# Four copies of an expert tile's code in TensorE's loop, put in the order widest first

## The chip, the cores and the metric

The kernel runs on one core of one Trainium2 chip. The metric is the device time of one execution in microseconds (us). Before the change the median of 3 runs is 2206.23 us, from 2205.37 to 2207.76 us.

## The reference

One encoder block on 1024 tokens of 1024 channels, in float32. A token mixer (gated short convolution beside multi-head latent attention, one output projection) is followed by a mixture of experts: the router picks 4 of 32 experts for each token, each expert is a clamped SwiGLU of width 1024, and the outputs are added, weighted by the gates.

```python
def moe_ffn(h, w_router, b_router, w_gate_up, b_gate_up, w_down, b_down):
    logits = hf @ w_router + b_router
    top_vals, top_idx = lax.top_k(logits, TOP_K)          # 4 of 32
    gates = jax.nn.softmax(top_vals, axis=-1)
    order = jnp.argsort(top_idx.reshape(-1))              # token rows sorted by expert
    xs, sizes = hf[order // TOP_K], jnp.bincount(...)
    gu = lax.ragged_dot(xs, w_gate_up, sizes) + b_gate_up[e_sorted]
    act = (clip(up) + 1.0) * (gate * jax.nn.sigmoid(SWIGLU_ALPHA * gate))
    out = lax.ragged_dot(act, w_down, sizes) + b_down[e_sorted]
    y = jax.ops.segment_sum(out * gate_of_row, token_of)
```

How many tokens each expert gets is known only on the chip, since the router decides it there.

## The kernel before, in words

Up to about 655 us the kernel computes the mixer and the router as straight-line code, in an order of steps that `schedule()` writes out. The rest is the mixture of experts. The token rows of each expert are cut into tiles of at most 160 (`SLOTS`). A table computed on the chip (lines 1220 to 1255) holds for each tile its expert and how many tokens it has (`held_i`), and `n_i` holds the number of tiles.

Every engine runs its own loop over the tiles (`expert_tiles`, lines 179 to 187): an outer loop over groups of `GROUP` = 6 tiles (line 183) that skips a group past the last tile (line 184), and an inner loop over the six (line 185). SyncE loads the weights of a tile in pieces of 1 MB, 12 per tile. GpSimd gathers the token rows of the next tile from DRAM and scatters the results of the tile before. VectorE transposes the gathered rows (line 1268), which lets TensorE begin a tile (`xT_ready`), and works on the products. ScalarE computes the sigmoids and the bias of the output.

TensorE reads the token count of the tile into a register (line 1036), goes past the tile if there are none (line 1038), waits for `xT_ready` (line 1041, attached to the compare that follows) and then chooses one of four copies of the tile's code by the count: the matmuls stream 128, 136, 148 or 160 token columns (`WIDTHS`, line 55). Such a copy is called a body here, and body 128 is the one of 128 columns. A body is itself a loop over the two halves of the expert's hidden channels (line 1029): each pass issues 64 matmuls of gate and up (`gate_up`, line 1003) and 32 of down (`down`, line 1019). In the trace each matmul shows as two weight loads and two matmul records.

The choice is written as nested `If`/`Else` by a recursive helper at lines 1043 to 1053. In TensorE's program that becomes, for each width but the last, a compare-and-branch (line 1046) that falls into the body below it when its condition holds, and otherwise jumps to the next compare behind that body. A body that is not the last ends in a jump to the end of the inner loop (line 1046 too, shown in the trace as COMPARE_BRANCH as well). The end of the inner loop (line 185) jumps back to its top.

TensorE's sequencer reads these instructions and fills a queue ahead of the array, so it deals with the end of one tile while the array still works on the last matmuls.

Of the kernel before, what the change touches and what calls it, by code (L numbers as in the profile page):

```python
# [54 lines left out]
WIDTHS = [P, P + 8, P + 20, SLOTS]  # L55
# [123 lines left out]
@contextmanager  # L179
def expert_tiles(eng, used):  # L180


    with eng.Fori(0, GROUPS * GROUP, GROUP) as first:
        with eng.If(first < used):
            with eng.Fori(first, first + GROUP) as t:
                yield t
# [27 lines left out]
def build(nc, I, out):  # L214
# [5 lines left out]
    with ctx:  # L220
# [574 lines left out]
        def _(pe):  # L795
# [198 lines left out]
            def gate_up(m, part, width):  # L994
                read, done = (gate_read, gate_done) if part == 0 else (up_read, up_done)
                pe.wait_ge(read, m * NH + NH)
                for s in range(2):
                    piece = 2 * part + s
                    pe.wait_ge(w_exp_in[piece], m * 16 + 16)
                    for c in range(NH):  # L1000
                        dst = bank[2 * part + c // 2][:, (c % 2) * SLOTS:(c % 2) * SLOTS + width]
                        for k in range(PART):
                            ins = mm(dst, w_gu[piece][:, k, c * P:(c + 1) * P], xT[:, PART * s + k, 0:width],  # L1003
                                     start=(s == 0 and k == 0 and c % 2 == 0), stop=(s == 1 and k == PART - 1),
                                     skip_group_check=True)
                        if s == 0 and c == NH - 1:
                            ins.then_inc(lo_done, 1)
                        if s == 1 and c % 2:
                            ins.then_inc(done, 1)

            def down(m, q, width):

                pe.wait_ge(w_exp_in[4 + q], m * 16 + 16)
                if q == 0:
                    pe.wait_ge(outT_ready, m * 8 + 8)
                pe.wait_ge(act_ready, m * 2 + q + 1)
                for kk in range(2):
                    for d in range(KD):
                        ins = mm(bank[4 + d // 3][:, (d % 3) * SLOTS:(d % 3) * SLOTS + width],  # L1019
                                 w_dn[q][:, kk, d * P:(d + 1) * P], actT[:, 2 * q + kk, 0:width],  # L1020
                                 start=(q == 0 and kk == 0 and d % 3 == 0), stop=(q == 1 and kk == 1),
                                 skip_group_check=True)
                ins.then_inc(down_done, 1)
# [3 lines left out]
            def expert_tile(t, width):  # L1027

                with pe.Fori(t * HALVES, t * HALVES + HALVES) as m:
                    gate_up(m, 0, width)  # L1030
                    gate_up(m, 1, width)
                    for q in range(2):
                        down(m, q, width)

            with expert_tiles(pe, n_tiles) as t:
                tokens = pe.value_load(held_i[0:1, bass.ds(t, 1)])

                with pe.If(tokens < 1):
                    pe.nop()
                with pe.Else():  # L1040
                    pe.wait_ge(xT_ready, t + 1)

                    def narrowest(widths):

                        if len(widths) > 1:
                            with pe.If(tokens < widths[0] + 1):
                                expert_tile(t, widths[0])
                            with pe.Else():
                                narrowest(widths[1:])
                        else:  # L1050
                            expert_tile(t, widths[0])

                    narrowest(WIDTHS)


        @block.vector
# [298 lines left out]
```

## Time and profile before

| what | value |
|---|---|
| median of 3 runs | 2206.23 us |
| the profiled execution's own time | 2206.78 us |
| its span in the trace | 2205.0 us |
| PE busy | 2078.0 us, 94% |
| PE weight loads busy | 1883.0 us, 85% |
| DVE, ACT, POOL busy | 738.2, 443.7, 563.1 us |
| chain that ended last, PE's share | 91% |
| DMA queue q8, kind instruction | 36 packets, 0.59 MB |

Times are from the start of the span. PE is TensorE's array, PEld its weight loads, and PEldq the rows of its sequencer, which are not counted as busy. "[x <-issue]" behind a row of the timeline is idle time of the array before that row in which it waited for nothing that the profile shows. A packet of the kind instruction is a piece of program being fetched for an engine's sequencer.

### The profile page before, as it was taken

The page shows a single profiled execution, that of the slowest core. Times are in us where ns is not written, and L with a number is a line of the kernel's source. Part 1 is how long each engine was busy: PE and PEld are TensorE (multiplying, and loading weights), DVE is VectorE, ACT ScalarE, POOL GpSimd, SP SyncE. Part 2 cuts the span into 40 slices and gives each one's busy share as a digit, 9 for nine tenths or more (in the row PEclk, how much of TensorE's full clock was granted, in tenths as well). Part 3 has the DMA queues.
Part 4 walks back from the last instruction along what each step waited for, and adds up shares of the span by engine and source line. Part 5 has one row for each costly group of instructions (what it writes and reads, how often), then busy time and mean ns, then how long its engine had stood idle before and what let it go on. Part 6 is the DMA issues. An engine that isn't in the chain of part 4 may idle for free.

```text
span 2205.0 us, 41908 instructions
## 1 busy us (share of the span) xinstructions
PE 2078.0 (94%) x15574; PEld 1883.0 (85%) x15575; DVE 738.2 (33%) x1949; ACT 443.7 (20%) x1078; POOL 563.1 (26%) x645
## 2 busy tenths in 40 slices
PE   7999999999968899999999999999999999999991
PEld 6777777745538899999999999999999999999991
DVE  1322333233443334234333333333233332343331
ACT  1333323232311111111111111111111111111110
POOL 2211111100233223322222322323223233232321
PEclk9999999999978999999999999999999999999996
DMA  7100000242517889999899999999999999999987
GB/s 251 40 10 11 10 11 1 80 131 47 145 39 228 268 281 310 313 297 304 270 305 277 310 289 298 310 284 289 301 312 318 308 272 283 321 315 319 306 284 88
DMA packets 305892, 486.97 MB, mean 221 GB/s; under 512 B 105920, under 2 KB 127200, under 8 KB 305792
## 3 DMA queue, kind: packets, MB, share of 16 engines
q1 hardware_dynamic: 247184, 437.28, 60.6%
q0 software_dynamic: 33376, 45.11, 9.9%
q10 hardware_dynamic: 25280, 3.85, 1.1%
q8 instruction: 36, 0.59, 0.1%
q14 instruction: 16, 0.13, 0.0%
HBM read 454.83 MB, written 35.84 MB: 223 GB/s over the span
## 4 chain that ended last, share of the span: by engine, by line
PE 91%; issue 2%; DVE 2%; ACT 1%; DMA 1%; POOL 1%; ACTq 0%; DVEq 0%; SPq 0%; POOLq 0%
PE psum L1003 43%; PE psum L1019 22%; PE psum L803 8%; PE psum L952 5%; PE psum L842 3%; PE psum L911 2%; PE psum L820 2%; PE psum L910 1%; PE psum L884 1%; PE psum L932 1%; PE psum L895 1%; DMA area<-in_w_in 1%; PE psum L982 1%; DVE area L1302 0%; DVE area L1297 0%
## 5 line engine op out<-in xcount | busy, mean ns | idle before, releaser
L1003 PE MATMUL psum<-area 128*128 128x128 f32 (+3 forms) x8192 | 980.2, 282 | 37.0 <-issue 18.9
L1003 PEld LDWEIGHTS psum<-area 128*128 128x128 f32 x8192 | 971.6, 192 | 42.4 <-issue 42.4
L1019 PE MATMUL psum<-area 128*128 128x128 f32 (+3 forms) x4096 | 496.4, 282 | 0.9
L1019 PEld LDWEIGHTS psum<-area 128*128 128x128 f32 x4096 | 484.5, 191 | 10.0 <-DVE area L1302 8.7
L1283 DVE TENSOR_SCALAR area<-psum,area 128x160 f32<-128x160 f32 x256 | 86.4, 380 | 615.6 <-PE psum L1003 615.6
L600 POOL DMA_INDIRECT sum_rows<-area x165 | 264.0, 1600 | 67.4 <-issue 40.2
L762 ACT ACTIVATE area<-area 128x320 f32<-128x320 f32 x128 | 60.4, 472 | 735.8 <-DVE area L1283 735.6
L803 PE MATMUL psum<-area 128*128 128x128 f32 x1536 | 176.8, 276 | 10.5 <-ACT area L681 4.0
L803 PEld LDWEIGHTS psum<-area 128*128 128x128 f32 x1536 | 173.3, 192 | 15.3 <-ACT area L677 5.8
L590 POOL DMA_INDIRECT area<-normed_rows,area x165 | 161.3, 977 | 61.5 <-issue 61.5
L585 POOL TENSOR_TENSOR area<-area 128x5 uint32<-128x5 uint32 x33 | 6.3, 190 | 617.4 <-DVE area L1268 590.4
L1297 DVE TENSOR_SCALAR area<-psum,area 128x160 f32<-128x160 f32 x256 | 86.5, 380 | 202.3 <-PE psum L1003 202.0
L785 ACT ACTIVATE area<-psum,area 128x160 f32<-128x160 f32 x256 | 76.5, 410 | 335.9 <-PE psum L1019 326.0
L952 PE MATMUL psum<-area 128*128 128x512 f32 x256 | 117.0, 611 | 0.0
L952 PEld LDWEIGHTS psum<-area 128*128 128x128 f32 x256 | 49.0, 197 | 55.9 <-issue 55.9
L1268 DVE STREAM_TRANSPOSE area<-area 128x256 f32<-128x256 f32 x165 | 90.2, 608 | 14.2 <-DMA area<-normed_rows,area 14.2
L1311 DVE TENSOR_TENSOR area<-area,psum 128x480 f32<-128x480 f32 (+1 forms) x96 | 51.7, 594 | 114.2 <-PE psum L1019 114.2
L597 POOL COPY area<-area 128x5 uint32 x33 | 6.2, 188 | 324.9 <-ACT area L768 324.9
L842 PE MATMUL psum<-area 128*128 128x384 f32 (+1 forms) x256 | 79.1, 468 | 2.1 <-DMA area<-in_w_in 1.7
L768 ACT ACTIVATE area<-area 128x256 f32<-128x256 f32 x165 | 69.6, 498 | 45.0 <-DVE area L1276 45.0
L820 PEld LDWEIGHTS psum<-consts,area 128*128 128x128 f32 x408 | 46.9, 143 | 36.6 <-issue 26.7
L574 POOL DMA_INDIRECT token_lists<-area x32 | 31.2, 974 | 177.0 <-DVE area L1081 169.7
(184 smaller groups left out, 1250.6 us busy)
## 6 DMA issues: line engine op xcount, KB each, us to landing
area<-in_w_gate_up SPq DMA_DIRECT2D x256, 1024.0 KB, 6.4
area<-in_w_down SPq DMA_DIRECT2D x128, 1024.0 KB
area<-in_w_in SPq DMA_DIRECT2D x3, 2048.0 KB, 21.5
area<-in_x SPq DMA_DIRECT2D x9, 512.0 KB, 4.0
area<-in_w_o SPq DMA_DIRECT2D x1, 4096.0 KB, 13.0
sum_rows<-area SPq DMA_DIRECT2D x32, 128.0 KB
normed_rows<-area SPq DMA_DIRECT2D x8, 512.0 KB, 3.1
out<-sum_rows SPq DMA_DIRECT2D x4, 1024.0 KB, 14.0
```

The lines of the kernel that those rows point to most:

```text
L590: g.indirect_dma_start(xg[:, k, :], None, hf_quarters, bass.IndirectOffsetOnAxis(ap=pick[:, k:k + 1], axis=0)).then_inc(gathered, 16)
L600: g.indirect_dma_start(acc_quarters, bass.IndirectOffsetOnAxis(ap=put[:, k:k + 1], axis=0), rows[:, k, :], None, compute_op=ALU.add).then_ ...
L785: A(outT[:, d, :], bank[4 + d // 3][:, (d % 3) * SLOTS:(d % 3 + 1) * SLOTS], ACT.Identity, bias=bdT[:, d, bass.ds(e, 1)]).then_inc(outT_re ...
L803: ins = mm(bk[:, f * P:(f + 1) * P], w_in[:, k, col + f * P:col + (f + 1) * P], hnT[:, k, :], start=(k == 0), stop=(k == KD - 1))
L820: ins = tr(bk[:, k * P:(k + 1) * P], part, ident)
L842: ins = mm(bk[:, 0:b - a], hnT[:, k, :], w_in[:, k, 3 * CONV + a:3 * CONV + b], start=(k == 0), stop=(k == KD - 1))
L952: ins = mm(bank[c], lhs, w_o[:, k, c * 512:(c + 1) * 512], start=(k == 0), stop=(k == 2 * NF - 1))
L1003: ins = mm(dst, w_gu[piece][:, k, c * P:(c + 1) * P], xT[:, PART * s + k, 0:width], start=(s == 0 and k == 0 and c % 2 == 0), stop=(s == 1 ...
L1019: ins = mm(bank[4 + d // 3][:, (d % 3) * SLOTS:(d % 3) * SLOTS + width], w_dn[q][:, kk, d * P:(d + 1) * P], actT[:, 2 * q + kk, 0:width], ...
L1268: ins = V.transpose(xT[:, :, 32 * k:32 * k + 32], xg[:, k, :].rearrange("p (r c) -> p c r", c=KD))
L1283: V.tensor_scalar(g_c[:, c, :], bank[j][:, (c % 2) * SLOTS:(c % 2 + 1) * SLOTS], bguT[:, NH * h + c, bass.ds(e, 1)], LIMIT, ALU.add, ALU.m ...
L1297: V.tensor_scalar(u_c[:, c, :], bank[2 + j][:, c * SLOTS:(c + 1) * SLOTS], bguT[:, NC + NH * h + 2 * j + c, bass.ds(e, 1)], -LIMIT, ALU.ad ...
```

## The change

The tree of `If`s tests for the widest body first instead of the narrowest. The four bodies and the number of instructions are the same; their order in TensorE's program turns from 128, 136, 148, 160 to 160, 148, 136, 128. Every tile still runs the body of the same width. Nothing changes for the other engines.

```diff
-                    def narrowest(widths):
+                    def widest(widths):
 
                         if len(widths) > 1:
-                            with pe.If(tokens < widths[0] + 1):
-                                expert_tile(t, widths[0])
+                            with pe.If(tokens > widths[-2]):
+                                expert_tile(t, widths[-1])
                             with pe.Else():
-                                narrowest(widths[1:])
+                                widest(widths[:-1])
                         else:
                             expert_tile(t, widths[0])
 
-                    narrowest(WIDTHS)
+                    widest(WIDTHS)
```

The first place is TensorE's entry into the tree, from the load of the token count (L1036) over the test for an empty tile (L1038) to the first matmuls behind the first compare (L1046). Before:

```order
L1036 TENSOR_LOAD area
L1038 COMPARE_AND_BRANCH
L1038 UNCONDITIONAL_BRANCH
L1041 REGISTER_ALU
L1046 COMPARE_AND_BRANCH
L1029 ISA
L1029 UNCONDITIONAL_BRANCH
L1029 ISA
L999 ISA
L1003 MATMUL psum<-area 128x128 x64
```

Now:

```order
L1046 COMPARE_AND_BRANCH
L1029 ISA
L1029 UNCONDITIONAL_BRANCH
L1029 ISA
L999 ISA
L1003 MATMUL psum<-area 128x160 x64
```

The first compare now has body 160 below it; a tile of 128 columns takes this jump and two more, over three bodies.

The second place is TensorE's program around the last compare, with the body behind it and the end of the inner loop (L185) and of the outer one (L184, L183). Before:

```order
L1046 UNCONDITIONAL_BRANCH
L1029 ISA
L1029 UNCONDITIONAL_BRANCH
L1029 ISA
L999 ISA
L1003 MATMUL psum<-area 128x160 x64
```

Now:

```order
L1046 UNCONDITIONAL_BRANCH
L1029 ISA
L1029 UNCONDITIONAL_BRANCH
L1029 ISA
L999 ISA
L1003 MATMUL psum<-area 128x128 x64
```

Behind the last body stand in both programs these rows:

```order
L1029 ISA
L1029 COMPARE_AND_BRANCH
L1048 UNCONDITIONAL_BRANCH
L185 ISA
L185 COMPARE_AND_BRANCH
L184 UNCONDITIONAL_BRANCH
L183 REGISTER_ALU
L183 COMPARE_AND_BRANCH
```

Body 128 now runs into the loop's end without a jump over other bodies, and body 160 has such a jump.

## Rows read from the trace of the kernel before

**Rows 1.** The page, part 1: busy us (share of the span) xinstructions

```profile
PE 2078.0 (94%) x15574; PEld 1883.0 (85%) x15575; DVE 738.2 (33%) x1949; ACT 443.7 (20%) x1078; POOL 563.1 (26%) x645
```

**Rows 2.** Groups by shape, PE, 400 to 2205 us: busy us, mean ns | idle before

```profile
L1003 PE MATMUL psum<-area 128*128 128x128 f32 x4608 | 526.0, 277 | 23.6 <-DVE area L1268 17.8 <-issue 5.5
...
L1003 PE MATMUL psum<-area 128*128 128x136 f32 x1536 | 182.9, 281 | 7.3 <-issue 7.3
L1003 PE MATMUL psum<-area 128*128 128x160 f32 x1024 | 140.8, 299 | 3.0 <-issue 3.0
L1003 PE MATMUL psum<-area 128*128 128x148 f32 x1024 | 130.6, 289 | 3.1 <-issue 3.1
```

**Rows 3.** Timeline of PE, tiles 0 to 3: start us, us, engine line [idle before]

```profile
671.85 17.22 PE L1003 MATMUL psum<-area 128*128 128x128 f32 x128 [17.80 <-DVE area L1268]
...
723.75 17.48 PE L1003 MATMUL psum<-area 128*128 128x136 f32 x128 [5.52 <-issue]
...
776.28 16.18 PE L1003 MATMUL psum<-area 128*128 128x128 f32 x128 [4.96 <-issue]
...
821.66 14.55 PE L1003 MATMUL psum<-area 128*128 128x128 f32 x128
```

**Rows 4.** Timeline of PE, starts of later tiles

```profile
909.44 15.09 PE L1003 MATMUL psum<-area 128*128 128x136 f32 x128 [0.32 <-issue]
...
1048.82 17.65 PE L1003 MATMUL psum<-area 128*128 128x160 f32 x128 [0.66 <-issue]
...
1092.38 8.86 PE L1019 MATMUL psum<-area 128*128 128x160 f32 x64
1101.08 14.45 PE L1003 MATMUL psum<-area 128*128 128x128 f32 x128
...
1748.89 16.37 PE L1003 MATMUL psum<-area 128*128 128x148 f32 x128 [0.56 <-issue]
```

**Rows 5.** Line 1046, five stretches: count, duration ns min/median/max, first and last start us

```profile
L1046 PEldq COMPARE_BRANCH  x1: 5252/5252/5252, 716.3 to 716.3; - x1
...
L1046 PEldq COMPARE_BRANCH  x1: 5087/5087/5087, 769.3 to 769.3; - x1
...
L1046 PEldq COMPARE_BRANCH  x76: 70/169/302, 819.7 to 2157.4; - x76
...
L1046 PEldq COMPARE_BRANCH  x1: 169/169/169, 863.5 to 863.5; - x1
...
L1046 PEldq COMPARE_BRANCH  x3: 202/202/215, 1047.7 to 1048.2; - x3
```

**Rows 6.** Line 999, 1100 to 1101 us: the sequencer's last instruction before a tile's matmuls

```profile
L999 PEldq FUSED_REGOPS  x1: 42/42/42, 1100.5 to 1100.5; - x1
```

**Rows 7.** DMA view, instruction packets in 0:630, 676:696, 717:722, 722:955, 955:1010

```profile
q8 instruction: 26, 0.43, 0.3%
...
q8 instruction: 2, 0.03, 0.6%
...
q8 instruction: 1, 0.02, 1.2%
...
q8 instruction: 4, 0.07, 0.1%
...
q8 instruction: 3, 0.05, 0.3%
```

**Rows 8.** Window of tile 0: stretch, five engines' busy us, PEclk, DMA share, GB/s

```profile
671.80:689.00 17.20, 17.15 (x128) 17.04 (x128) 5.49 (x15) 4.34 (x8) 6.13 (x10) 0.84 0.62 190
```

**Rows 9.** DMA view, 655:676 and then 696:717: packets; list read, us to landing

```profile
DMA packets 1649, 0.67 MB, mean 32 GB/s; under 512 B 1488, under 2 KB 1488, under 8 KB 1648
...
area<-token_lists ACTq DMA_DIRECT2D x8, 1.2 KB, 1.7
...
DMA packets 3881, 6.89 MB, mean 328 GB/s; under 512 B 859, under 2 KB 1283, under 8 KB 3880
...
area<-token_lists ACTq DMA_DIRECT2D x4, 1.2 KB, 4.3
```

## The prediction

> **What bounds the kernel.** I read the page first: TensorE is busy for 94% of the span [rows 1], so what moves the time is what moves TensorE. The groups by shape give the tiles: a pass over a body streams 128 matmul records of line 1003 and a tile has two passes, so 4608, 1536, 1024 and 1024 records are 18 tiles of 128 columns, 6 of 136, 4 of 148 and 4 of 160, 32 in all [rows 2]. No tile changes its width, so the matmuls cost what they did. The change can only act between tiles, and there the timeline is to be read for the idle time in brackets. Two gaps stand out, 5.52 us before tile 1 and 4.96 us before tile 2 [rows 3]; later a tile of 128 columns behind another has a gap of 0.04 us and no bracket, and one of 136, 148 or 160 behind a 128 has 0.32, 0.56 and 0.66 us [rows 4].
>
> The sequencer's rows on line 1046 explain both kinds. A jump there takes 202 to 215 ns (the three into the tile of 160 at 1048 us), the jump behind a body 169 ns, a compare that isn't taken about 70 ns, and none of the 76 behind tile 1 takes over 302 ns. But the jump behind tile 0 took 5252 ns and the one behind tile 1 5087 ns [rows 5]. In the first of these stalls exactly one instruction packet was moved (717 to 722 us), so the jump waited for code [rows 7].
>
> **Which code is at hand.** 26 packets of 0.43 MB came before 630 us, 16 KB each. Outside the loop stand 15574 less 32 x 384 / 2, or 3286 matmul records [rows 1], with their weight loads 6572 instructions, so a packet is a block of about 253. A pass is 384 instructions, a body one and a half blocks, the loop a little over six. If I number blocks by packets, the loop's top lies late in block 26, the second compare in 28, the third in 29, the last body's start in 31, the loop's end in 32. That fits the later packets if entering a block fetches the next one and no more: two in tile 0's first pass (28 and 29), then the jump to the end (32) and the block behind it, one while body 136 runs (30), the second stalled jump and the block behind it, and three around body 148 at 955 us [rows 7]. These sum to the page's 36, so in the 15 us in which TensorE waited for its first tile nothing was fetched ahead. From 1010 us on nothing is fetched at all: the whole loop is held. Until then a block that no one has run into or next to isn't there.
>
> **The change, tile boundaries first.** Compared with a 128 behind a 128, the entry into 136 costs 0.28 us (0.32 less 0.04), into 148 0.52, into 160 0.62 [rows 4]. The change mirrors these: 160 costs nothing extra, 148 0.28, 136 0.52, 128 0.62. So 128 and 136 lose 0.62 and 0.24 us, 160 and 148 gain as much. Body 128 also loses its jump to the end (169 ns and some 0.05 us to the next instruction, 0.22), and body 160 gets one. The sequencer has no slack behind a 128, as the gap shows. Behind a 160 it has 0.48: its last instruction starts at 1100.5 and takes 0.04, and some 0.05 us later it is ready, against a first matmul at 1101.08 [rows 4, 6]. Before a 160 the gain is capped by the real gap, 0.66 plus 0.16 by which a modelled end (1092.38 + 8.86 = 1101.24) lies behind the possible start (1101.08) [rows 4]. Over the 31 boundaries, as the timeline orders the tiles:
>
> - 128 behind 128, 8 times 0.62 - 0.22: +3.20. Behind 136, 3 times 0.62: +1.86. Behind 148, 2 times: +1.24. Behind 160, 4 times 0.62 + 0.22 - 0.48: +1.44.
> - 136 behind 128, 5 times 0.24 - 0.22: +0.10. Behind 148, once: +0.24.
> - 148 behind 128, once -0.46; behind 136, 3 times -0.24: -0.72.
> - 160 behind 128, 3 times -0.82: -2.46. Behind 148, once: -0.62.
>
> Sum +3.8 us. The compares wait for `xT_ready`, but no boundary names VectorE except the first, so nothing new waits there; SyncE, ScalarE, GpSimd and VectorE have the same programs, and their work, which waits for TensorE's counts, moves with it.
>
> The Trainium skill ("Advanced Engine Details and Errata", section Control Flow Timing) gives some 108 ns for a compare-and-branch and 51 ns for an unconditional one. By these, an estimate from that page, the same table would sum to about +1.2 us instead of +3.8. The rows above show about 70 ns when it falls through and over 200 when it jumps, and here nearly all added ones jump, so the rows decide.
>
> **The two stalls that go.** Body 128 now runs into the loop's end, and at tile 0's end block 32 was fetched when block 31 was entered. So the gap before tile 1 falls from 5.52 to 0.32, that before tile 2 from 4.96 to 0: 10.16 us. With them goes a loss of clock. TensorE had been granted half its speed after each stall: tile 1's first 128 matmuls took 17.48 us against 15.09 for the same work at 909 us, tile 2's 16.18 against 14.55 for tile 3 [rows 3, 4]: 2.39 + 1.63 = 4.02. Together -14.2 us. If their cover is wrong and the jump behind tile 1 still finds its target gone, 5 to 7 us of it stay.
>
> **The stalls that come.** Tile 0 has 128 columns [rows 3]. Before, its entry was one compare that fell through. Now it is three jumps, to blocks 28, 29 and 31, and only 27 is at hand. Each target must be fetched: 28 outright, 29 as the block next to 28 that is only being asked for when the jump comes, 31 outright. TensorE's array is idle here, no queued matmuls cover it, and the first matmul waits for all three. The clock is low there anyway: tile 0's first pass ran at 0.84 of full speed behind 17.80 us of idle [rows 3, 8], so I count nothing more for it; by the losses above 1 us either way is possible.
>
> The price of one is not shown for this moment. The nearest rows are the two stalls, 5.25 and 5.09 us, with weights streaming at over 300 GB/s; at tile 0 the DMA queues carry a tenth of that (32 GB/s), and a list read that lands in 4.3 us under load lands in 1.7 there [rows 9]. That bounds a fetch from 5.25 down to 5.09 - 2.6, or 2.5 us. A single packet should meet less of that queueing than a read of many small ones, so I stay near the stalls and take 4.6 us: 3 x (4.6 + 0.05) less the 0.12 of the compare that fell through gives +13.8 us.
>
> **Sum.** +3.8 - 14.2 + 13.8 = +3.4 us against the profiled execution's own 2206.78 us: 2210.2. The median of the three runs is 0.55 below it, which gives 2209.7; I say 2210.0. A measurement of this kernel can tell about 0.2%, 4.4 us, from no change.
>
> **Rivals.**
> - Forecast, 0.50: three stalls of 4.1 to 5.1 us at tile 0. The sum is then +1.9 to +4.9 us; it passes 4.4 only with a price over 4.9 us, so of this 0.37 counts as the same and 0.13 as slower.
> - The third jump waits twice, 0.27: block 30 is being fetched when the jump to 31 comes, and its fetch goes out only when that one is done. No row shows a miss during a fetch; the jumps right behind the first stall went on at once, but their targets were held. Four prices instead of three: +8.0 us, 2214.5, slower.
> - Fetches are cheap on idle queues, 0.12: for it speaks the list read, against it that the two stalls differ by only 0.17 us. At 2.5 to 4.1 us the sum is -2.9 to +1.9, the same; 2203.5 at the least.
> - The other side, 0.08, faster: bodies passed over are already at hand at tile 0, because what lies ahead is fetched in more than one block while TensorE waits for `xT_ready`, so at most the first jump stalls. Place: the three jumps at 671 us. Price: one stall of 4.65 and two jumps of 0.25, less 0.12, 5.0 us in place of 13.8, so -5.4 us, 2201. It decides when the entry costs less than 5.9 us in all. Against it: the two stalls of before happened although the fetcher had had over 40 us.
> - Every jump over a body stalls in every tile, 0.01: the loop isn't held, only the blocks around the present one. 70 jumps into bodies and 14 behind them at some 5 us make over 400 us, about 2600. The 76 jumps of at most 302 ns and the lack of packets behind 1010 us speak against it [rows 5, 7]. The Trainium skill says this ("Runtime: NRT & Kernel Launch", section Instruction fetch mechanics): a taken branch whose target is outside a window of two blocks forces a fetch, and nothing is cached. The trace agrees with its block of 16 KB and its stall, not with its window.
> - That the change does nothing is excluded by TensorE's program; 0.02 stays for other causes that make it slower, such as bodies 148 and 160 stalling on first use.
>
> **How the numbers follow.** The prediction is the forecast's, 2210.0 us. The range, 2203.5 to 2216.0, takes in the low bound of a fetch and the doubled third jump with the clock's 1 us, and leaves out the other side and the 2600. Faster 0.09, same 0.37 + 0.12 = 0.49, slower 0.13 + 0.27 + 0.01 + 0.02, rounded to 0.42.
>
> **What would show it.** Right: three COMPARE_BRANCH rows of line 1046 between 671 and 690 us with 4 to 5 us each and a first matmul near 685.7; no bracket over 1 us before tiles 1 and 2, and their first passes at 15.1 and 14.6 us; 0.44 us before a 128 behind a 128, none before a 160 behind a 128; some 32 packets on q8, none behind tile 0. Wrong: a first matmul before 677 us, stalls of line 1046 in later tiles, a slow clock in tiles 1 or 2 without a stall, or a third jump of about 9 us.

## The result: slower by 0.5%, outside the range

The changed kernel takes 2221.16 us (median of 11 runs, 2207.65 to 2224.39), the kernel before 2208.11 us in runs beside it (11 runs, 2205.37 to 2212.41). The ratio is 1.0054, with a 95% interval of 1.0041 to 1.0068. I had forecast 2210.0 us and no measurable change, and 2221.16 lies 5.2 us above the top of my range. The profiled execution took 2218.12 us, with a span of 2216.3 us, against 2206.78 and 2205.0 before.

The page of the changed kernel, parts 1 and 3: TensorE's work, and the packets of program.

```profile
PE 2074.7 (94%) x15574; PEld 1878.3 (85%) x15575; DVE 738.6 (33%) x1949; ACT 443.2 (20%) x1078; POOL 562.0 (25%) x645
...
q8 instruction: 39, 0.64, 0.1%
```

Against [rows 1] the counts are equal and PE's busy time is 3.3 us lower, so all of the 11.3 us, and 3 more, is idle time of the array. This execution is 3 us below the median of its kernel; the medians are 13.1 us apart, and what is read below accounts for 11.3 of them.

The groups by shape of the changed kernel, PE, 400 to 2217 us (busy us, mean ns | idle before):

```profile
L1003 PE MATMUL psum<-area 128*128 128x128 f32 x4608 | 523.6, 276 | 37.8 <-issue 37.8
...
L1003 PE MATMUL psum<-area 128*128 128x136 f32 x1536 | 183.5, 282 | 11.8 <-issue 11.8
L1003 PE MATMUL psum<-area 128*128 128x160 f32 x1024 | 140.7, 299 | 0.3 <-issue 0.3
L1003 PE MATMUL psum<-area 128*128 128x148 f32 x1024 | 130.6, 289 | 1.8 <-issue 1.7
```

Read against [rows 2]: the idle time ahead of 160 and 148 fell by 2.7 and 1.3 us, as the swap of the order should do. Ahead of 128 it rose by 14.2 us, at tile 0 alone by 11.8. Ahead of 136, where the stall of 5.52 us was to vanish, it rose by 4.5.

The timeline of PE in the changed kernel, starts of tiles 0 to 3 and of three later ones (start us, us, engine line [idle before]):

```profile
681.87 15.94 PE L1003 MATMUL psum<-area 128*128 128x128 f32 x128 [29.62 <-issue]
...
736.62 18.11 PE L1003 MATMUL psum<-area 128*128 128x136 f32 x128 [9.65 <-issue]
...
785.66 14.55 PE L1003 MATMUL psum<-area 128*128 128x128 f32 x128 [0.83 <-issue]
...
829.84 14.55 PE L1003 MATMUL psum<-area 128*128 128x128 f32 x128 [0.47 <-issue]
...
918.02 15.09 PE L1003 MATMUL psum<-area 128*128 128x136 f32 x128 [0.31 <-issue]
...
1056.78 17.58 PE L1003 MATMUL psum<-area 128*128 128x160 f32 x128
...
1109.41 14.55 PE L1003 MATMUL psum<-area 128*128 128x128 f32 x128 [0.27 <-issue]
```

Against [rows 3]: the first matmul behind 29.62 us of idle time instead of 17.80, a gap of 9.65 us before tile 1 instead of 5.52, and none to speak of before tile 2 instead of 4.96. Tile 1 is again granted a reduced clock (18.11 us for what takes 15.09 at 918 us), tile 2 the full one. Later tiles stand as the table of boundaries had them: 0.47 before a 128 behind a 128, no bracket before a 160, 0.27 before a 128 behind a 160.

The rows of line 1046 in the changed kernel: the entry, the first jump behind tile 0, the whole of that boundary, and everything later (count, duration ns min/median/max, first and last start us):

```profile
L1046 PEldq COMPARE_BRANCH  x3: 3011/3317/5227, 669.7 to 676.2; - x3
...
L1046 PEldq COMPARE_BRANCH  x1: 5683/5683/5683, 726.5 to 726.5; - x1
...
L1046 PEldq COMPARE_BRANCH  x3: 70/3885/5683, 726.5 to 736.2; - x3
...
L1046 PEldq COMPARE_BRANCH  x92: 70/202/308, 782.8 to 2126.3; - x92
```

The entry stalls three times, 11.6 us in all. Behind tile 0, which now runs into the loop's end, the jump that stalls is no longer the one to the end. It is the first compare of tile 1, from the loop's top over body 160 to the second compare, and then the second compare's jump over body 148: 5.68 and 3.89 us. Both targets had been fetched 50 us earlier, for tile 0. The third compare of tile 1 takes 70 ns: it falls through into body 136.

The packets of program (q8) in the changed kernel, 665 to 690, 690 to 720 and 720 to 800 us; there is none from 800 us on:

```profile
q8 instruction: 5, 0.08, 1.7%
...
q8 instruction: 1, 0.02, 0.2%
...
q8 instruction: 7, 0.11, 0.7%
```

Six packets for the way through the tree at tile 0, then seven more at tile 1. By the numbering of the prediction the first six are blocks 28 to 33 and the seven are 27 and then 28 to 33 **once more** (the numbers are inferred from the order of the jumps; the trace shows only the packets).

### The profile page after: what moved, and what is told of

It reads as the page before. It is cut to its first block, busy times and chain, and to the rows that moved or that the text cites. A ratio compares the mean times of both kernels' runs of the same rounds, so it can differ in the third digit from the quotient of the medians.

```text
span 2216.3 us, 41924 instructions
## 1 busy us (share of the span) xinstructions
PE 2074.7 (94%) x15574; PEld 1878.3 (85%) x15575; DVE 738.6 (33%) x1949; ACT 443.2 (20%) x1078; POOL 562.0 (25%) x645
## 4 chain that ended last, share of the span: by engine, by line
PE 90%; issue 3%; DVE 2%; DMA 1%; ACT 1%; POOL 1%; ACTq 0%; DVEq 0%; SPq 0%; POOLq 0%
PE psum L1003 42%; PE psum L1019 22%; PE psum L803 8%; PE psum L952 5%; PE psum L842 3%; PE psum L911 2%; PE psum L820 2%; PE psum L910 1%; PE psum L884 1%; PE psum L932 1%; PE psum L895 1%; DMA area<-in_w_in 1%; PE psum L982 1%; DVE area L1302 0%; DVE area L1297 0%
## 5 line engine op out<-in xcount | busy, mean ns | idle before, releaser
L1003 PEld LDWEIGHTS psum<-area 128*128 128x128 f32 x8192 | 969.2, 192 | 57.8 <-issue 57.8
L1019 PEld LDWEIGHTS psum<-area 128*128 128x128 f32 x4096 | 484.5, 191 | 10.0 <-DVE area L1302 8.7
L803 PEld LDWEIGHTS psum<-area 128*128 128x128 f32 x1536 | 173.3, 192 | 14.6 <-ACT area L677 5.8
L952 PEld LDWEIGHTS psum<-area 128*128 128x128 f32 x256 | 49.2, 198 | 56.4 <-issue 56.4
L842 PEld LDWEIGHTS psum<-area 128*128 128x128 f32 x256 | 48.9, 194 | 31.7 <-issue 4.6
## 6 DMA issues: line engine op xcount, KB each, us to landing
area<-in_w_o SPq DMA_DIRECT2D x1, 4096.0 KB, 13.1
```

What stands on the lines that cost most here:

```text
L803: ins = mm(bk[:, f * P:(f + 1) * P], w_in[:, k, col + f * P:col + (f + 1) * P], hnT[:, k, :], start=(k == 0), stop=(k == KD - 1))
L842: ins = mm(bk[:, 0:b - a], hnT[:, k, :], w_in[:, k, 3 * CONV + a:3 * CONV + b], start=(k == 0), stop=(k == KD - 1))
L952: ins = mm(bank[c], lhs, w_o[:, k, c * 512:(c + 1) * 512], start=(k == 0), stop=(k == 2 * NF - 1))
```

## Experiments

Packets of q8 are counted over the whole run: 36 before, 39 in the changed kernel. Diffs are against the kernel named.

### 1 and 2. The wait for the tokens moved behind the compares

The wait for `xT_ready` sits on the first compare, so in the changed kernel all of the entry's fetches begin only when the tokens are there. Here each body waits for itself: the tree is passed while TensorE has nothing to do. The second kernel is the same edit on the old order, as a control.

```diff
             def expert_tile(t, width):
 
+                pe.wait_ge(xT_ready, t + 1)
                 with pe.Fori(t * HALVES, t * HALVES + HALVES) as m:
...
-                    pe.wait_ge(xT_ready, t + 1)
```

> The changed kernel, with TensorE's wait for xT_ready moved from in front of the first compare into each body, so that the three jumps of tile 0 and their fetches happen from 656 us on, while the rows of tile 0 are still gathered. Theory A (the jumps of the entry lay blocks 28 to 33 over their neighbours in the instruction memory, whenever they happen, and tile 1 must fetch 27 to 30 again): the 11.6 us of the entry (3.3 + 3.0 + 5.2) vanish behind the wait, the first matmul is near 672 us, but the gap of 9.65 us before tile 1 and its slow clock stay: 11 us less than the changed kernel, about 2210 us. Theory B (the blocks are lost only because the jumps of the entry fall together with something at 670 us, the gather of tile 1 or the end of the wait): the gap before tile 1 goes too, about 2198 us.

> The kernel before with the same move of the wait: a control, since tile 0 there takes no jump. Both theories: no change, ratio 1.000 within 0.002, first matmul near 672 us, stalls of about 5.2 and 5.0 us before tiles 1 and 2.

Measured in the changed order: 2209.68 us, ratio to before 1.0012 (1.0002 to 1.0021). Its timeline of PE, tiles 0 to 2:

```profile
673.25 16.86 PE L1003 MATMUL psum<-area 128*128 128x128 f32 x128 [18.83 <-DVE area L1268]
...
728.65 17.07 PE L1003 MATMUL psum<-area 128*128 128x136 f32 x128 [9.39 <-issue]
...
776.63 14.55 PE L1003 MATMUL psum<-area 128*128 128x128 f32 x128 [0.82 <-issue]
```

Its rows of line 1046 at the entry:

```profile
L1046 PEldq COMPARE_BRANCH  x3: 3527/3658/5227, 656.9 to 664.2; - x3
```

The three stalls at the entry are no shorter (12.4 us in all), but now they lie ahead of 670 us, and the first matmul waits for VectorE again. That takes 11.5 us off the median (2221.16 to 2209.68). The two were measured at different times; each against the kernel before that ran beside it, the difference is 10.7 us (13.1 less 2.4). That is the price of the entry. The gap before tile 1 stays at 9.4 us, so it has nothing to do with how late the entry is. The control gives 2208.22 us, ratio 1.0001 (0.9992 to 1.0011): in the old order the wait's place is worth nothing.

### 3. The same, with the compares held apart

The third jump of the entry took 5.2 us instead of 3.3. Here the second compare waits for the tokens' list and the third for the gathered rows, so that the block fetched ahead should have landed before the next jump. The diff is against the changed order of experiment 1.

```diff
                         if len(widths) > 1:
+                                if len(widths) == 4:
+                                    pe.wait_ge(list_read, 1)
+                                if len(widths) == 3:
+                                    pe.wait_ge(gathered, 16 * G)
```

> As e1_wait_in_body, with waits between the jumps that only tile 0 feels: the second compare waits for list_read of 1 (660 us), the third for gathered of 80 (668.6 us), so that the jump to block 31 comes when block 30 has long arrived. Theory A (the place of a missed block is set by the block that the jump leaves): the gap before tile 1 stays at 8 to 10 us, first matmul 672 to 673 us, about 2210 us. Theory C (the loss comes from block 30 being in flight when 31 is asked for): the gap before tile 1 falls under 1 us and its clock is whole, 12 us less, about 2198 us.

Measured: 2212.89 us, ratio 1.0025 (1.0015 to 1.0036), 39 packets. Rows of line 1046 at the entry:

```profile
L1046 PEldq COMPARE_BRANCH  x3: 2307/3303/3773, 658.2 to 671.5; - x3
```

And tile 1 in its timeline of PE:

```profile
730.40 16.63 PE L1003 MATMUL psum<-area 128*128 128x136 f32 x128 [9.63 <-DMA area<-normed_rows,area]
```

The doubled wait is gone: the three now take 3.8, 2.3 and 3.3 us, none over 5. Only the third jump was really held apart, by 6.3 us; the second started 0.9 us behind the end of the first, and its 2.3 us fit the rest of a fetch under way. The third is the one that counts: 5.2 us without the pause, 3.3 with it. So a jump that comes while the block ahead is still being fetched waits for that fetch first, the mechanism of my rival of 0.27. But the gap before tile 1 is unchanged, so the overlap of two fetches is not what loses the code.

### 4. Body 128 second

Order 160, 128, 136, 148: tile 0 jumps once on the way in, and again at its end. The helper `choose`, not shown, writes each compare for the width that stands first.

```diff
...
-                    widest(WIDTHS)
+                    choose([SLOTS, P, P + 8, P + 20])
```

> The changed kernel with the bodies in the order 160, 128, 136, 148: tile 0 takes one jump (block 26 to 28) and ends in a jump over two bodies to block 32. Theory A: one stall of 3.3 us at the entry; block 28 was laid over 27, so tile 1's first jump to 28 stalls again, and the jump to 32 stalls 5 us too, a gap of 5 to 10 us before tile 1. Rival (a missed block goes behind the one already fetched ahead, 27 stays): only the jumps to 32 stall, as in the kernel before, 5 us each before tiles 1 and 2. Either way the entry costs 3.3 in place of 11.6 us and the boundaries into 128 about 0.22 us in place of 0.42 more than before: 2208 to 2214 us.

Measured: 2229.31 us, ratio 1.0112 (1.0094 to 1.0131), the worst of all. Its rows of the compares from the end of tile 0 to the start of tile 1:

```profile
L1051 PEldq COMPARE_BRANCH  x4: 70/4320/7692, 725.3 to 743.4; - x4
```

And tile 1 in its timeline:

```profile
743.83 16.66 PE L1003 MATMUL psum<-area 128*128 128x136 f32 x128 [16.63 <-issue]
```

The jump to the loop's end misses (5.27 us) and then the two over bodies miss as well (7.69 and 3.37): 16.6 us before tile 1, where I had expected 5 to 10. Again one of the two targets over bodies had been used by tile 0 and was not held at tile 1. The time is 15 us above the 2208 to 2214 that I expected. The profiled execution is the fastest of the four, 8 us below their median, so those 8 us were not read.

### 5 and 9. Old order, and an empty turn of the loop that walks the tree

If code has to be run past before it is held, it can be run past while TensorE waits for its first tokens. The loop gets one turn more ahead of tile 0. The word read as its count is a large number, so all compares jump, and a compare in front of the last body jumps over that one. Each body waits for itself as in experiment 1, and its numbers are shifted by one turn.

```diff
-            with expert_tiles(pe, n_tiles) as t:
-                tokens = pe.value_load(held_i[0:1, bass.ds(t, 1)])
+            counts_from = tabs_i.rearrange("p c n -> p (c n)")[:, 2 * TABLE - 1:]
+            with expert_tiles(pe, n_tiles + 1) as u:
+                tokens = pe.value_load(counts_from[0:1, bass.ds(u, 1)])
...
                         else:
-                            expert_tile(t, widths[0])
+                            with pe.If(tokens < SLOTS + 1):
+                                expert_tile(u, widths[0])
```

> The kernel before (bodies in the order 128, 136, 148, 160) with one empty turn of TensorE's tile loop ahead of tile 0: it takes the three jumps from compare to compare, jumps over the last body and comes back, all while the rows of tile 0 are gathered, and runs no matmul. The wait for xT_ready stands in the bodies, and the last body has a compare in front of it (0.14 us for a tile of 160). Slot theory (eight slots in a ring; the next block goes to the slot behind the present one, a missed target two slots on, but on the first jump out of the straight run one slot on, over block 27): afterwards 26, 28, 29, 31, 32 and 33 are held, tile 0 fetches 27 to 29 ahead without a stall, and the jumps to block 32 find it. 39 instruction packets in all, no bracket over 1 us before tiles 1 and 2, their first passes 15.1 and 14.6 us, first matmul 1 to 3 us later than before: 12 us less than the kernel before, 2194 to 2197 us. Rival (a block so far away is only kept when its body has run): the stalls before tiles 1 and 2 stay, 2207 to 2210 us.

> The kernel of the run with the walk in the old order, once more, with more rounds, beside the walk in the changed order: 2191 to 2194 us, ratio to before 0.993 to 0.995, no gap over 1 us before tiles 1 and 2. If the gain of the first time was chance, the time is within 0.2% of before.

Measured: 2192.49 us, ratio 0.9936 (0.9919 to 0.9953), and the second time 2196.45 us, 0.9951 (0.9938 to 0.9965). The first is 1.5 us below what I expected, the second 2.5 us above, and both beat both kernels. Since experiment 2 found nothing in the wait's place alone, the gain is the empty turn's. The compares of the first of the two runs in the empty turn, and the same line from then on:

```profile
L1048 PEldq COMPARE_BRANCH  x3: 3407/3811/5167, 655.1 to 662.4; - x3
...
L1048 PEldq COMPARE_BRANCH  x82: 70/169/311, 672.6 to 2142.4; - x82
```

Its timeline of PE, tiles 0 and 1:

```profile
673.12 16.34 PE L1003 MATMUL psum<-area 128*128 128x128 f32 x128 [20.61 <-issue]
...
718.88 15.09 PE L1003 MATMUL psum<-area 128*128 128x136 f32 x128 [0.26 <-issue]
```

The stalls of [rows 5] are gone, and with them the slow clock behind them. The first matmul is 1.3 us later than in [rows 3]; in the second measurement it came at 677.25 us, which is 4.1 of the 5.0 us between the two profiled spans.

The walk does not save the second fetch, it hides it. Behind the 6 packets of the walk 7 more come here too: 3 while tile 0's body runs (672 to 716 us), 1 in tile 1 (730 to 762 us) and 3 between 945 and 1000 us, around the first tile of 148 columns. With the 26 before they make 39, as in the changed kernel, but here no jump waits for one: none behind 672 us takes over 311 ns.

### 6 and 7. An empty turn that jumps straight to the loop's end

The same extra turn, but it skips the whole tree with one compare on the loop's number, in the old order and in the changed one.

```diff
+            with expert_tiles(pe, n_tiles + 1) as u:
+                with pe.If(u > 0):
+                    tokens = pe.value_load(counts_from[0:1, bass.ds(u, 1)])
```

> The kernel before with an empty turn that jumps at once to the end of the loop (block 32) and back, and so fetches only 32 and 33 ahead. Each tile has one compare more, about 0.14 us, 4 us in all. Slot theory: 32 goes to 27's slot, 27 to 29 then overwrite 32 and 33, and tile 0's end must fetch 32 again: both stalls of about 5 us stay, 39 packets, 2209 to 2213 us. Rival (a fetched block stays until the memory is full; something else cost tile 1 its code): the stall before tile 1 goes, that before tile 2 too, 36 packets or fewer, 2196 to 2200 us.

> The changed kernel (order 160, 148, 136, 128) with the wait in the bodies and the same empty turn to the end of the loop. Slot theory: 32 and 33 take two slots, 27 then goes to its own slot behind 26, so the jumps of tile 0 lay 28, 29, 30, 31 and 32, 33 in a row behind it, and nothing is overwritten that is needed: 35 packets in all, the stalls before tile 1 (9.4 us with the wait in the bodies) are gone and its clock is whole. The entry itself has one stall more and ends near 675 us. 2204 to 2208 us with 4 us for the compare more per tile. Rival (tile 1's stalls come from jumping over bodies that have not run): gap of 9 us before tile 1 stays, 38 or more packets, about 2217 us.

Measured in the old order: 2213.02 us, ratio 1.0031 (1.0020 to 1.0043), 38 packets. Tiles 1 and 2 in its timeline:

```profile
723.77 17.08 PE L1003 MATMUL psum<-area 128*128 128x136 f32 x128 [5.90 <-issue]
...
776.32 17.48 PE L1003 MATMUL psum<-area 128*128 128x128 f32 x128 [5.38 <-issue]
```

The loop's end had been fetched by a jump of 3.78 us in the empty turn, and the jump to it stalls behind tile 0 all the same (5.44 us), after only 4 packets in all. So a block once fetched need not be there at its second use.

In the changed order: 2213.86 us (2201.29 to 2218.92 in 10 runs), ratio 1.0018 (0.9999 to 1.0037), 41 packets. Tile 1 in its timeline:

```profile
732.16 17.38 PE L1003 MATMUL psum<-area 128*128 128x136 f32 x128 [8.82 <-issue]
```

I had expected this gap to be gone, and 2204 to 2208 us. I had worked with a finer model by then: eight places in a ring, in which a jump's target is put at a certain distance from the present block. Its 39 packets for experiment 5 were counted, but for these two it gives 39 and 35, where 38 and 41 were counted. So the model is not shown, and where a fetched block is put stays open. One caution: four of the ten runs in the changed order took 2201.29 to 2208.05 us, while the profiled one took 2217.74. So the 41 packets and the gap of 8.8 us are those of one of the six longer ones, and what the other four did was not seen.

### 8. The walk, in the changed order

The kernel of experiment 5 with the tree of the changed kernel. The word read in the empty turn is brought below 129 by a remainder, which leaves real counts as they are, so that again all compares jump.

```diff
+                    tokens = count_or_list % (SLOTS + 1)
...
-                            with pe.If(tokens < widths[0] + 1):
-                                expert_tile(u, widths[0])
+                            with pe.If(tokens > widths[-2]):
+                                expert_tile(u, widths[-1])
...
-                            with pe.If(tokens < SLOTS + 1):
+                            with pe.If(u > 0):
```

> The changed order (160, 148, 136, 128) with the empty turn of the run with the walk ahead of tile 0: the three compares are met and the last body is jumped over while TensorE would wait anyway, so every jump target has been fetched once before a tile needs it. Theory A (what the change costs beyond 4 us is instruction fetches, at the entry and behind tile 0): no gap over 1 us before tiles 1 and 2, first matmul near 673.2 us, and the time is that of the walk in the old order, 2192.5, plus the table of the tile boundaries (3.8), plus one compare more ahead of body 128 (18 x 0.07 = 1.3) and one register instruction per tile (32 x 0.05 = 1.6, part of it hidden): 2197 to 2200 us. Rival (the gap before tile 1 has another cause than missing code, such as the order itself): a gap of 8 to 10 us stays before tile 1 and the time is 2207 to 2211 us.

Measured: 2219.11 us, ratio 1.0056 (1.0042 to 1.0069), 39 packets, some 20 us above what I expected. Its compares in the empty turn, at the entry of tile 0, and later:

```profile
L1049 PEldq COMPARE_BRANCH  x3: 3511/3790/5167, 658.4 to 665.8; - x3
...
L1049 PEldq COMPARE_BRANCH  x3: 3250/4903/6601, 676.0 to 686.0; - x3
...
L1049 PEldq COMPARE_BRANCH  x95: 70/202/217, 736.2 to 2127.8; - x95
```

Its timeline of PE, tiles 0 to 2:

```profile
691.52 16.23 PE L1003 MATMUL psum<-area 128*128 128x128 f32 x128 [35.80 <-issue]
...
737.35 15.09 PE L1003 MATMUL psum<-area 128*128 128x136 f32 x128 [0.45 <-issue]
...
783.34 14.55 PE L1003 MATMUL psum<-area 128*128 128x128 f32 x128 [0.81 <-issue]
```

This is the run that tells most. The gap before tile 1 is gone, and instead the entry of tile 0 pays: 6.6, 3.3 and 4.9 us for jumps whose targets had been asked for 18 to 20 us earlier. The first of them is like the first behind tile 0 in the changed kernel (5.7 us, 6.8 in experiment 10), and longer than the first fetch of any target on idle queues (2.9 to 3.9 us, 5.2 when doubled). So in this order the stall does not belong to tile 1. It belongs to the **second way** through the tree (a way is one passage of the sequencer over the compares, in an empty turn or for a tile), whichever turn that is. The same number of packets, 39, comes either way. In the old order the second way, tile 0 in experiment 5, met no stall: it makes no jump over a body on its way in, its jump to the loop's end finds its target, and the code that is fetched again there comes while a body runs. Both orders fetch it twice behind a walk; only in the changed one do jumps have to wait for it.

### 10. The changed kernel again

> The changed kernel itself, profiled a second time. If the stall before tile 1 follows from where code lies, it is 9 to 10 us again behind two jumps, and the packets are 39 again. If it is a race between fetches (one of eleven runs took 2207.65 us), a second profile can show another gap (0.3 or 5 us) and another count of packets.

Measured: 2222.40 us, ratio 1.0055 (1.0036 to 1.0074), again 39 packets, first fetches of 3.7, 3.2 and 4.9 us, jumps of 6.8 and 3.2 us behind tile 0. Tile 1 in its timeline:

```profile
740.59 17.95 PE L1003 MATMUL psum<-area 128*128 128x136 f32 x128 [10.05 <-issue]
```

### 11. Two walks, in the changed order

The kernel of experiment 8 with one more empty turn; the numbers taken from the turn's number shift with it.

```diff
-            with expert_tiles(pe, n_tiles + 1) as u:
+            with expert_tiles(pe, n_tiles + 2) as u:
...
-                            with pe.If(u > 0):
+                            with pe.If(u > 1):
```

> The changed order with two empty turns of the loop ahead of tile 0 instead of one. With one, the compares stalled in the empty turn (3790, 3511, 5167, 3280 ns) and again at tile 0 (6601, 3250, 4903 ns), then no more. Theory D (the code fetched on the first way through the tree is displaced by the refetching on the second way, once; on the third all is held): the first empty turn stalls as before, the second stalls at 6.6, 3.3 and 4.9 us, and at tile 0 no compare takes over 0.35 us; first matmul near 691 us, no gap over 1 us before tiles 1 and 2, 39 packets, 2218 to 2221 us. Rival (code is only held once a body has been run in full, or once the weights' loads have begun; the number of ways through the tree has nothing to do with it): the compares stall a third time at tile 0, the first matmul comes at 705 us or later, there are 45 packets or more and the time is 2230 us or more.

Measured: 2227.32 us, ratio 1.0086 (1.0069 to 1.0103), 39 packets. Its compares in the first empty turn, in the second, at the entry of tile 0, and later:

```profile
L1049 PEldq COMPARE_BRANCH  x3: 2911/3795/4992, 655.7 to 662.6; - x3
...
L1049 PEldq COMPARE_BRANCH  x3: 3514/5179/6587, 672.7 to 682.9; - x3
...
L1049 PEldq COMPARE_BRANCH  x3: 208/208/211, 693.0 to 693.6; - x3
...
L1049 PEldq COMPARE_BRANCH  x95: 70/202/217, 740.5 to 2136.1; - x95
```

The jump over the last body, in the first empty turn and in the second:

```profile
L1054 PEldq COMPARE_BRANCH  x1: 3465/3465/3465, 667.6 to 667.6; - x1
...
L1054 PEldq COMPARE_BRANCH  x1: 3490/3490/3490, 688.1 to 688.1; - x1
```

The third way through takes 208 to 211 ns a jump, without any body having run. Code is lost on the second way and held from the third, and the number of packets does not grow. Nor is it a matter of the hour: the third way comes at 693 us here, while the second of the changed kernel still stalls at 726. The time is 6 us above what I had put on record. I had left out the fourth jump of the second walk, which stalls too (3.49 us), and with it the first matmul is 3.5 us later than I said. The rest lies behind it: against experiment 8 the first 128 matmuls take 1.3 us more (17.48 against 16.23), and from tile 2 to the last tile the starts spread by 3.9 us more (787.82 to 2137.06 against 783.34 to 2128.66), in gaps whose cause was not looked for.

## Why the prediction was wrong

The differences are read between the two profiled executions, from the starts of tiles in the timelines (span 2216.3 less 2205.0, +11.3 us).

- **The stalls that go, -14.2 us: this step failed.** The gap before tile 2 and the clock behind it went as I said (4.96 to 0.83 us, 16.18 to 14.55). The gap before tile 1 was to fall from 5.52 to 0.32 and rose to 9.65; its clock was to recover and got 0.6 us worse. Over the three boundaries behind tiles 0 to 2, gaps and clock sum to +4.13 - 4.13 + 0.43 + 0.63 - 1.63 = -0.57, of which +1.04 is the boundary table's (0.02, 0.62 and 0.40); so -1.6 us in place of -14.2. I had covered tile 1 with two sentences: block 32 is fetched on entering 31, and blocks 28 and 29 had been fetched at the entry. The first held, since no jump to the loop's end stalls. The second was never said, only assumed: that what has been fetched stays. The runs show that on the second way through the tree it does not (9.65 us before tile 1, and 14.8 us of stalls at tile 0 in experiment 8), and on the third it does (at most 211 ns a jump in experiment 11). My caveat that 5 to 7 us of a stall could stay was about tile 2's side and too small; the stall that came had two misses.
- The hint was in the trace of before. After tile 0 had jumped over bodies to the loop's end, its code was not held for tile 1's end: the second stall of [rows 5], with the same target as the first. I had explained both stalls by 32 and 33 having been asked for, and did not ask why block 32 had to be fetched **twice**. A target that misses twice within 53 us says that fetched code is lost.
- **The stalls that come, +13.8 us: right in kind, mis-sized.** The three jumps stall with 3.32, 3.01 and 5.23 us, 11.6 in all; the gap ahead of the first matmul grew by 11.8 (17.80 to 29.62), and experiment 1 prices it at 10.7 to 11.5. A fetch on the idle queues costs 2.9 to 3.9 us, not 4.6: I should have gone by the list read of [rows 9], not stayed near the loaded stalls. The third is doubled, as the rival of 0.27 said; its mechanism is right (experiment 3) while its sum of four prices of 4.6 is not. The clock gave back 1.3 us in tile 0 (17.22 to 15.94), a little more than the 1 us that I had left for it, and the work ahead of the loop ended 1.8 us earlier in this execution. Net of both, +8.7 us against 13.8.
- **Tile boundaries, +3.8 us: right.** From the start of tile 3 to the start of the last tile the changed kernel takes 3.2 us longer (2126.91 less 829.84, against 2115.57 less 821.66), where the table gives 3.8 less the 1.04 of the three boundaries before, 2.8. The groups by shape show both signs of it. The start of the last tile, before and then changed:

```profile
2115.57 14.55 PE L1003 MATMUL psum<-area 128*128 128x128 f32 x128
...
2126.91 14.55 PE L1003 MATMUL psum<-area 128*128 128x128 f32 x128 [0.61 <-issue]
```

- The sum: +8.7 - 1.6 + 1.0 + 3.2 = +11.3 us. Against the forecast's +3.4 the entry is 5.1 lower (1.8 of it the earlier start), the stalls 12.6 higher, the boundaries 0.4 higher. That the result missed the range by only 5 us is in part luck: the entry's price, put too high, made up for some of the failed step.
- The prediction's count of 3286 records outside the loop is 15574 less 32 x 384; the division by two that is printed there does not belong to it, and the count is right.
- Of the other rivals: the cheap fetches were nearest to the truth on the price, but their sum rested on the same step. The other side (bodies at hand at tile 0) was wrong, with 11.6 us of stalls where it needed less than 5.9. That every jump stalls in every tile is excluded: 92 rows behind 780 us take at most 308 ns. The Trainium skill ("Runtime: NRT & Kernel Launch", section Instruction fetch mechanics) gives TensorE 128 KiB for instructions, and a window of two blocks to jump in. The loop, a little over six blocks of 16 KB, is about 100 KB and is held from the third way on, which agrees with the first figure and not with the second (92 rows of at most 308 ns, half of them at 202 ns or more, as jumps over bodies take). It does not tell why code fetched on the first way is missed on the second.

What stays open: where a block is put, and so why exactly the second way loses what the first has fetched. Experiments 6 and 7 speak against a ring of eight places filled by a fixed distance. Whether timing decides too is also open, since runs of one kernel differ by more than 10 us.

## What to carry to other kernels

A loop with bodies chosen by `If` pays for its code in its first turns, and what the first turn has fetched by jumps can be fetched again later, so a jump target that was used once isn't yet a covered one. Count the stalls by way through the code, not by place, and look for a target that misses twice. The second fetch costs nothing when the engine runs into the code while it works, and 3 to 8 us a jump when it jumps there. If the engine has idle time ahead of the loop, spend it on an empty turn through the tree and keep the wait for data behind the compares: here that took 10.6 and 14.2 us (0.5 and 0.6%) off in the order that runs straight into the body of the first tile, and nothing clear in the other (ratios to before of 1.0056 with the walk and 1.0055 without, measured side by side), where the second way still falls on a real tile.

## What the runs showed of the hardware that I had not expected

- A jump to code that isn't held cost 2.9 to 3.9 us while the DMA queues were nearly idle (2.3 us in experiment 3, where the fetch was probably under way), 5.1 to 5.4 us with weights streaming, and about 5 us on idle queues if the block ahead was still being fetched; the first miss of a second way took 5.4 to 7.7 us.
- In the changed order fetched code was lost once and then held to the end: 39 packets whether the tree was walked none, one or two times ahead of tile 0.
- Behind a stall of 5 to 17 us of the array the granted clock is reduced (0.50 from 736.6 to 740 us in the changed kernel, the lower of its two levels, and 0.83 over the first pass of that tile), and the next 128 matmul records take 16.0 to 18.1 us instead of 14.55 to 15.09: 1.4 to 3.0 us more per stall. The longest, 16.6 us in experiment 4, cost no more than the short ones (1.6 us).
- Some runs of the changed kernel took about 12 us less than the others (3 of 19 over both measurements, 2207.65 to 2209.13 us), and experiment 7 spread over 17.6 us. No profile of the changed kernel fell on such a run, so whether the stall before tile 1 is missing in them wasn't seen.
